# First block marked from the ranks alone, weighted slots turned block by block, shift added by the first scatter

## The reference

```python
g_prob = softmax(xt @ w_rg + b_rg); g_val, g_idx = top_k(g_prob, 1)          # 1 of 4 groups
e_logits = (xt @ w_re + b_re).reshape(-1, 4, 4); e_val, e_loc = top_k(e_logits[g_idx], 2)
e_w = softmax(e_val) * g_val                                                 # two weights per token
for e in range(16):
    out += combine[:, e] * ((silu(xt @ w_gate[e]) * (xt @ w_up[e])) @ w_down[e])
```

## Time and profile before

| what | value |
|---|---|
| three runs | 1733.82, 1735.91 (median), 1738.47 us |
| profiled execution | 1732.53 us, of it the span 1730.8 us |
| busy share of the span | TensorE 91%, weight load 61%, VectorE 54%, ScalarE 30%, GpSimd 3% |
| mean granted TensorE clock | 0.964 of full speed |
| memory traffic | 547.28 MB, mean 316 GB/s |
| gate and up matmuls (line 1048) | 6016 records, 371.2 us |
| last chain by engine | TensorE 74%, SyncE's queue 15%, DMA 4%, VectorE 4% |

### The profile page before, as it was taken

How to read it: one execution, slowest core, us unless ns; L and a number is a source line. 1 busy time by engine, 2 the same in 40 slices (tenths; PEclk the granted TensorE clock), 3 DMA queues, 4 the chain that set the end, 5 groups by cost and what they waited for, 6 DMA issues and landing times.

```text
span 1730.8 us, 35353 instructions
## 1 busy us (share of the span) xinstructions
PE 1568.8 (91%) x14820; PEld 1060.2 (61%) x14821; DVE 926.5 (54%) x1444; ACT 522.8 (30%) x602; POOL 48.4 (3%) x36
## 2 busy tenths in 40 slices
PE   8999999997999999966699999999989999986664
PEld 8999899885444444322299999998744444432221
DVE  7658655646555555431477476466475554552234
ACT  4552543423121212110264543533232112111011
POOL 0004000000000000000000040000000000000000
PEclk9999999999999999988899999999999999998887
DMA  9553455588999999999975544555999999999996
GB/s 305 202 179 126 160 167 189 195 337 351 420 422 422 418 419 400 424 421 422 410 235 180 162 144 160 166 191 195 392 373 421 421 422 422 419 423 422 422 421 269
DMA packets 139206, 547.28 MB, mean 316 GB/s; under 512 B 23060, under 2 KB 26360, under 8 KB 88568
## 3 DMA queue, kind: packets, MB, share of 16 engines
q1 hardware_dynamic: 138740, 546.13, 80.9%
...
HBM read 544.04 MB, written 2.10 MB: 316 GB/s over the span
## 4 chain that ended last, share of the span: by engine, by line
PE 74%; SPq 15%; DMA 4%; DVE 4%; issue 2%; DVEq 1%; ACT 0%; ACTq 0%
PE ps L808 24%; PE ps L1048 14%; PE ps L965 10%; SPq L432 9%; PE ps L1066 7%; SPq L436 5%; PE ps L805 5%; PE ps L1031 4%; PE ps L1012 3%; DMA room<-in_w_down_dram 3%; PE ps L1020 1%; DVE room L1118 1%; DVE h L1118 1%; PE ps L934 1%; PE ps L884 1%
## 5 line engine op out<-in xcount | busy, mean ns | idle before, releaser
L1048 PE MATMUL ps<-room 128*32 128x256 f32 x6016 | 371.2, 404 | 96.6 <-DMA room<-in_w_up_dram 91.1
L1118 DVE TENSOR_TENSOR w_lo<-room,w_hi 128x2048 fp32r<-128x2048 f32 (+1 forms) x121 | 281.4, 2335 | 232.9 <-ACT w_hi L520 232.4
L1048 PEld LDWEIGHTS ps<-room 128*32 128x32 f32 x6016 | 201.2, 116 | 282.0 <-DMA room<-in_w_up_dram 111.6
L808 PE MATMUL ps<-hT_hi,w_hi 128*128 128x256 f32 x1152 | 330.9, 287 | 0.9 <-DVE w_lo L1118 0.7
L808 PE MATMUL ps<-hT_hi,w_lo 128*128 128x256 f32 x1152 | 327.8, 285 | 0.0
L808 PE MATMUL ps<-hT_lo,w_hi 128*128 128x256 f32 x1152 | 327.7, 284 | 0.0
L520 ACT ACTIVATE w_hi<-room 128x2048 fp32r<-128x2048 f32 x120 | 228.3, 1914 | 228.4 <-PE ps L808 102.0
L1118 DVE TENSOR_TENSOR h<-h,ps 128x512 f32<-128x512 f32 x376 | 232.9, 681 | 98.0 <-PE ps L1031 97.5
L808 PEld LDWEIGHTS ps<-hT_hi,w_hi 128*128 128x128 f32 x1152 | 223.0, 194 | 3.8 <-issue 2.4
L808 PEld LDWEIGHTS ps<-hT_hi,w_lo 128*128 128x128 f32 x1152 | 223.0, 194 | 0.7 <-issue 0.5
L808 PEld LDWEIGHTS ps<-hT_lo,w_hi 128*128 128x128 f32 x1152 | 222.9, 194 | 0.0
...
## 6 DMA issues: line engine op xcount, KB each, us to landing
room<-in_w_gate_dram SPq DMA_DIRECT2D x128, 1024.0 KB, 19.0
room<-in_w_up_dram SPq DMA_DIRECT2D x128, 1024.0 KB, 21.0
room<-in_w_down_dram SPq DMA_DIRECT2D x128, 1024.0 KB, 16.5
...
```

The lines of the kernel that those rows point to most:

```text
L808: last = eng.matmul(ps[:, b + o // 2, (o % 2) * T:(o % 2) * T + T], w_[:, o * P:o * P + P], x_[:, kk, :], start=opens and o % 2 == 0, stop ...
L1048: last = eng.matmul(ps[r0:r0 + BLK, 0, 0:2 * P], xe[:, x0:x0 + BLK], unit_gu(u)[:, :, k, c * P:c * P + P], start=(i == 0 and k == 0), stop ...
L1118: return eng.tensor_tensor(o, a, b, op)
```

## The change

- `first_hot`: right after the ranks VectorE compares the ranks within expert 0 with 0 to 31 and multiplies by the membership in expert 0. Counting, `tab_first`, sort and positions come behind it, positions and the further marks behind `take_rows`.
- The spreading of positions and weights over partitions, `rows` and `place_rows` go. For each block VectorE makes `weighed` (a one-hot of slots times weights, `weigh`), TensorE turns it with 8 matmuls (`place_block`, behind `scatter(g, 1)`), and ScalarE copies the result to `place`.
- The shift is no longer loaded to all partitions. `yraw` is cleared, four rows of it get `ln1_b`, and `place` is 1 for slot 0 of each group and 0 elsewhere, so that the scatter of block 0 adds the shift to every token.
- The gain's load moves from ahead of the units to behind the ninth. The two gain multiplications are split around `hidden(g0)`.
- `h_k` is made in two steps, the first ahead of the first half's logits; `hT_r` moves to other room for that. Two filler calls instead of nine stand behind the ranks. GpSimd's clearing of the pads waits for `tab_ready` instead of `place_last`.

```diff
 eng.wait_ge(mix_split.sem, mix_split.at(l, 4))
-for m, v in enumerate((ln1_g, ln1_b)):
-    eng.dma_start(gb[:, m, :], v[l:l + 1].to_broadcast([P, D])).then_inc(gb1_loaded.sem, 16)
 def weights(w, e):
...
     e, i = u // PER_E, u % PER_E
+    if u == SLOTS:
+        eng.wait_ge(yraw_zero.sem, yraw_zero.at(l, 1))
+        eng.dma_start(gain_1, ln1_g[l:l + 1].to_broadcast([P, D])).then_inc(gb1_loaded.sem, 16)
+        eng.dma_start(yraw[0:P:BLK, :], ln1_b[l].rearrange("(c n) -> c n", c=4)).then_inc(gb1_loaded.sem, 16)
...
     half_evac(0, b)
+by_features(0)
 logits_evac(0)
...
 logits_evac(1)
-for t in range(NT):
-    eng.activation(h_k[:, t], h[:, t, :].rearrange("a (p k) -> a k p", k=KD), ACT.Copy
-                   ).then_inc(hk_ready.sem, 1)
+by_features(1)
 eng.wait_ge(ex_in.sem, ex_in.at(l, 1))
...
 copy_of(first_gathered.sem, first_gathered.at(l, 1), xrow, 3, first_rows.sem)
-eng.wait_ge(gain_done.sem, gain_done.at(l, 1))
-eng.wait_ge(spread_done.sem, spread_done.at(l, 1))
-eng.activation(rows.rearrange("p r t -> p (r t)"), banks(4, 2), ACT.Copy).then_inc(spread_ready.sem, 1)
 eng.wait_ge(tab_first.sem, tab_first.at(l, 1))
...
     copy_of(hmT_done, g + 1, hmT, 1, hmT_ready)
+    eng.wait_ge(place_done, g + 1)
+    eng.activation(place, ps[:, 1, P:P + T], ACT.Copy).then_inc(place_ready, 1)
     copy_of(y_done, g + 1, yraw, 2, y_ready)
...
 eng.matmul(ps[:, 1, 32:48], ones[:], M[:, 2, 1, :], start=False, stop=True).then_inc(ranks_done.sem, 1)
-keep_busy(9, 7)
+keep_busy(2, 7)
 def gather(ready, count, done):
...
     if t == 0:
-        eng.wait_ge(place_ready, g + 1)
+        eng.wait_ge(place_ready, g + l + 1)
         eng.wait_ge(y_ready, g + 1)
...
                    start=True, stop=True, tile_position=(r0, 0)).then_inc(sc_done, 1)
+def place_block(g):
+    eng.wait_ge(weighed_ready, g + 1)
+    for t in range(NT):
+        for c in range(4):
+            r0 = BLK * c
+            last = eng.matmul(ps[r0:r0 + BLK, 1, P + t * P:P + t * P + P], weighed[:, t, :], ident[:],
+                              start=True, stop=True, tile_position=(0, r0))
+    last.then_inc(place_done, 1)
...
             scatter(g, 1)
+            place_block(g)
...
-for i in range(2):
-    for j, col in ((0, pos12), (1, wts)):
-        for t in range(NT):
-            last = eng.matmul(banks(4, 2)[:, (2 * j + i) * T + t * P:(2 * j + i) * T + t * P + P],
-                              col[:, i, t, :].to_broadcast([P, P]), ident[:], start=True, stop=True)
-last.then_inc(spread_done.sem, 1)
...
-eng.wait_ge(place_last.sem, place_last.at(l, 1))
+eng.wait_ge(place_ready, g0 + nb + l + 1)
 eng.wait_ge(y_ready, g0 + nb + 1)
...
             eng.wait_ge(added, (g0 + nb) * 8 + c + 13)
-        eng.matmul(ps[:, 4 - 4 * t + c, :], place_l[r0:r0 + BLK, t * P:t * P + P], yraw[r0:r0 + BLK, :],
+        eng.matmul(ps[:, 4 - 4 * t + c, :], place[r0:r0 + BLK, t * P:t * P + P], yraw[r0:r0 + BLK, :],
                    start=True, stop=True, tile_position=(r0, 0)).then_inc(sc_last.sem, 1)
...
                     ).then_inc(hr_dve.sem, 1)
+eng.wait_ge(lgp_done.sem, lgp_done.at(l, NT))
+eng.memset(yraw, 0.0).then_inc(yraw_zero.sem, 1)
 eng.wait_ge(logits_done.sem, logits_done.at(l, 1))
...
 eng.wait_ge(ranks_done.sem, ranks_done.at(l, 1))
+counts = ps[:, 1, 0:NT * 16].rearrange("p (t e) -> p t e", t=NT)
+tt(hot, iota[:].rearrange("p (o s) -> p o s", o=1).to_broadcast([P, NT, BLK]),
+   counts[:, :, 0:1].to_broadcast([P, NT, BLK]), ALU.is_equal)
+eng.drain()
+tt(hot, hot, M[:, 2, :, 0:1].to_broadcast([P, NT, BLK]), ALU.mult).then_inc(first_hot.sem, 1)
 tt(over[:], ps[:, 1, 32:48].rearrange("p (e o) -> p e o", o=1).to_broadcast([P, 16, T // BLK - 1]),
...
-tt(sorted_blocks, sorted_by, tab[:, 0:1, :].to_broadcast([P, 16, 16]), ALU.mult)
-eng.drain()
-eng.tensor_reduce(tab[:, 1, :], sorted_blocks, AX.X, ALU.add)
-eng.drain()
-eng.scalar_tensor_tensor(pos, tab[:, 1:2, :].to_broadcast([P, NT, 16]), float(BLK),
-                         ps[:, 1, 0:NT * 16].rearrange("p (t e) -> p t e", t=NT), ALU.mult, ALU.add)
-eng.tensor_copy(block_iota, iota[:])
-eng.drain()
-tt(t32[:], M[:, 0:2], pos.rearrange("p (o t) e -> p o t e", o=1).to_broadcast([P, 2, NT, 16]), ALU.mult)
-eng.drain()
-eng.tensor_reduce(pos12, t32[:], AX.X, ALU.add)
-eng.drain()
-def mark(ready):
-    tt(hot_2[:], block_iota.rearrange("p (o u s) -> p o u s", o=1, u=1).to_broadcast([P, 2, NT, BLK]),
-       pos12.to_broadcast([P, 2, NT, BLK]), ALU.is_equal)
-    eng.drain()
-    tt(hot, hot_2[:, 0], hot_2[:, 1], ALU.add).then_inc(ready, 1)
-    ts(block_iota, block_iota, float(BLK), None, ALU.add)
-    eng.drain()
-mark(first_hot.sem)
-ts(tab[:, 1, :], tab[:, 1, :], carry[:], None, ALU.add)
 eng.tensor_reduce(total[:, 0, :], tab[:, 0, :], AX.X, ALU.add)
+eng.tensor_copy(tab[:, 1, 0:1], carry[:])
+tt(tab[:, 1, 1:2], tab[:, 0, 0:1], carry[:], ALU.add)
 eng.drain()
...
                          ).then_inc(tab_first.sem, 1)
-eng.wait_ge(ex_ready.sem, ex_ready.at(l, 1))
-eng.tensor_reduce(gval, ex[:, :, 0:4], AX.X, ALU.add)
-ts(wts[:, 1], ex[:, :, 4:5], 1.0, None, ALU.add)
-eng.drain()
-eng.scalar_tensor_tensor(gval, gval, ALPHA, wts[:, 1], ALU.mult, ALU.mult)
-eng.drain()
-eng.reciprocal(wts[:, 0], gval)
-eng.drain()
-tt(wts[:, 1], wts[:, 0], ex[:, :, 4:5], ALU.mult).then_inc(wts_ready.sem, 1)
+tt(sorted_by, key.rearrange("p (o n) -> p o n", o=1).to_broadcast([P, 16, 16]),
+   key.rearrange("p (e o) -> p e o", o=1).to_broadcast([P, 16, 16]), ALU.is_gt)
+eng.drain()
+tt(sorted_blocks, sorted_by, tab[:, 0:1, :].to_broadcast([P, 16, 16]), ALU.mult)
+eng.drain()
 def take_rows(done, count):
...
     tt(x4, x4, b_, ALU.add).then_inc(xe_ready, 1)
+take_rows(first_turned.sem, first_turned.at(l, 1))
+eng.tensor_reduce(tab[:, 1, :], sorted_blocks, AX.X, ALU.add)
+eng.drain()
+eng.scalar_tensor_tensor(pos, tab[:, 1:2, :].to_broadcast([P, NT, 16]), float(BLK), counts, ALU.mult, ALU.add)
+ts(block_iota, iota[:], float(BLK), None, ALU.add)
+eng.tensor_copy(place_iota, iota[:])
+eng.drain()
+tt(t32[:], M[:, 0:2], pos.rearrange("p (o t) e -> p o t e", o=1).to_broadcast([P, 2, NT, 16]), ALU.mult)
+ts(tab[:, 1, :], tab[:, 1, :], carry[:], None, ALU.add)
+eng.drain()
+eng.tensor_reduce(pos12, t32[:], AX.X, ALU.add)
+eng.drain()
+def slots(iota_):
+    return tt(hot_2[:], iota_.rearrange("p (o u s) -> p o u s", o=1, u=1).to_broadcast([P, 2, NT, BLK]),
+              pos12.to_broadcast([P, 2, NT, BLK]), ALU.is_equal)
+def mark():
+    slots(block_iota)
+    eng.drain()
+    tt(hot, hot_2[:, 0], hot_2[:, 1], ALU.add).then_inc(hot_ready, 1)
+    ts(block_iota, block_iota, float(BLK), None, ALU.add)
+    eng.drain()
+def weigh():
+    slots(place_iota)
+    eng.drain()
+    tt(hot_2[:], hot_2[:], wts.to_broadcast([P, 2, NT, BLK]), ALU.mult)
+    ts(place_iota, place_iota, float(BLK), None, ALU.add)
+    eng.drain()
+    tt(weighed, hot_2[:, 0], hot_2[:, 1], ALU.add).then_inc(weighed_ready, 1)
+eng.wait_ge(first_gathered.sem, first_gathered.at(l, 1))
+mark()
+eng.wait_ge(ex_ready.sem, ex_ready.at(l, 1))
+eng.tensor_reduce(gval, ex[:, :, 0:4], AX.X, ALU.add)
+ts(wts[:, 1], ex[:, :, 4:5], 1.0, None, ALU.add)
+eng.drain()
+eng.scalar_tensor_tensor(gval, gval, ALPHA, wts[:, 1], ALU.mult, ALU.mult)
+eng.drain()
+eng.reciprocal(wts[:, 0], gval)
+eng.drain()
+tt(wts[:, 1], wts[:, 0], ex[:, :, 4:5], ALU.mult)
 def add_block(g, t):
...
     tt(hmid, sgate, ps[:, 0, P:2 * P], ALU.mult).then_inc(hm_ready, 1)
-def place_rows():
-    eng.scalar_tensor_tensor(place, rows[:, 0, :], slot_col, rows[:, 2, :], ALU.is_equal, ALU.mult)
-    eng.scalar_tensor_tensor(place_2, rows[:, 1, :], slot_col, rows[:, 3, :], ALU.is_equal, ALU.mult)
-    eng.drain()
-    tt(place, place, place_2, ALU.add).then_inc(place_ready, 1)
-    ts(slot_col, slot_col, float(BLK), None, ALU.add)
-take_rows(first_turned.sem, first_turned.at(l, 1))
-eng.wait_ge(first_gathered.sem, first_gathered.at(l, 1))
-mark(hot_ready)
 eng.wait_ge(gb1_loaded.sem, gb1_loaded.at(l, 32))
 eng.wait_ge(hk_ready.sem, hk_ready.at(l, NT))
-tt(h[:, 0, :], h[:, 0, :], gb[:, 0, :], ALU.mult)
-tt(h[:, 1, :], h[:, 1, :], gb[:, 0, :], ALU.mult).then_inc(gain_done.sem, 1)
-eng.tensor_copy(slot_col, slot_of[:])
+tt(h[:, 0, :], h[:, 0, :], gain_1, ALU.mult)
+ts(place, slot_of[:].to_broadcast([P, T]), 0.0, None, ALU.is_equal).then_inc(place_ready, 1)
+eng.wait_ge(tab_first.sem, tab_first.at(l, 1))
+g0, nb = expert_row(eng, 1, 0), expert_row(eng, 4, 0)
 tt(carry[:], carry[:], total[:, 0, :], ALU.add)
...
 eng.drain()
+hidden(g0)
+tt(h[:, 1, :], h[:, 1, :], gain_1, ALU.mult)
 for r0, r1 in ((0, 2), (2, 3)):
...
 tt(tabi[:, 3, FIXED:], tabf[:, 0, FIXED:], tabf[:, 1, FIXED:], ALU.add).then_inc(tab_ready.sem, 1)
-eng.wait_ge(spread_ready.sem, spread_ready.at(l, 1))
-eng.memset(place, 0.0).then_inc(place_ready, 1)
-eng.wait_ge(tab_first.sem, tab_first.at(l, 1))
-g0, nb = expert_row(eng, 1, 0), expert_row(eng, 4, 0)
-hidden(g0)
-tt(h[:, 0, :], h[:, 0, :], gb[:, 1, :], ALU.add)
```

(7 more changed lines are left out.)

48 lines of the change are left out of this document (22 added, 26 removed).

## The result

The change makes the kernel slower by 0.3%: 1743.2 us against 1736.3 us (medians of 14 runs each on one chip), ratio 1.0032, 95% interval 1.0020 to 1.0044, so +3.5 to +7.6 us with +5.6 us in the middle (the medians alone differ by 6.9 us). The forecast was 1746 us, +10.3 us: direction and range held, the size was nearly twice that of the interval's middle.

The account below looks back on a forecast made before the run. TensorE was taken to bind from the first block to the last two-block expert, transfers afterwards. Layer 0: -3.0 + 16 x 0.50 = +5.0 us; layer 1: -1.7 + 14 x 0.50 = +5.3 us; +10.3 us, 1746.2 us, range 1737 to 1754 us.

Parts of the forecast that it names:

- Start of block 0: Head of each expert stage: marks without table, sort and positions let block 0 start 3.5 us earlier in each layer.
- rival 4: Head: the first block is not earlier, as the gather waits for the second feature copy or registers; +7 us more, 1753 us; 5%.
- Block 0: First expert block: VectorE's moved work and gain wait take back 0.5 us in layer 0 and 1.8 us in layer 1.
- from the end of the row scaling ... 15.7 us: Block 0: VectorE's operations up to its first add, listed one by one, sum to 15.7 us.
- Rival 3: Block 0's gate/up runs partly at half clock after seven of nine filling calls go; 2 to 3 us more, +12 us, 1748 us; 6%.
- About 1 us of it passes VectorE's list: Block 0: of the 2 to 3 us that gate/up would lose at half clock, about 1 us outlasts VectorE's work.
- The turned slots: Each block: eight added TensorE matmuls (16 records) behind the second scatter cost 0.50 us, over 16 blocks in layer 0, 14 in layer 1.
- Nothing added there is hidden: Blocks up to the last two-block expert: TensorE works end to end, so added matmuls show in full, 0.50 us a block.
- Behind the deciding block: From block 17 (layer 0) or 15 (layer 1) only transfers count, so +5.0 and +5.3 us pass to the layer's end.
- Transfers as the limit in the blocks before (1): Expert stage: transfers bind instead of TensorE, so the earlier start and removed losses give -9.8 us, 1726 us; 7%.
- Block 0 getting short (2): VectorE reaches its first add before TensorE needs it; block 0 takes 17 us instead of 23.3 and 22.4, 1732 to 1737 us; 9%.
- Weight loads in the open (5): Turning matmuls: each of 16 weight loads stands alone at 116 ns, 1.9 us a block, +52 us, 1788 us; 3%.

Follow-up runs that it names:

- the two transposes: Changed kernel with each block's place turned by two 128 x 128 transposes instead of eight matmuls: 1743.1 us, 1.0030 to the kernel before.
- one exchanged pair of lines: Changed kernel with the second half's gain multiplication ahead of block 0's gating instead of behind it: 1737.3 us, 0.9997 to the kernel before.

## Why the forecast was right in sign and too large

**Start of block 0** (3.5 us): 3.2 and 3.4 us. The two small operations, the gather and the row scaling came as reckoned; the missing part is the registers that TensorE reads ahead of the turn, a piece of rival 4. The second feature copy ended at 407.08 us, 1.3 us ahead of the gather at 408.36 us, near the 1.5 us of the forecast. The tenth unit was issued 2.9 us behind the start and not 2 us, since gate/up was slow: 2.2 us earlier in place of 3.5.

**Block 0** (longer by 0.5 and 1.8 us; layer 0's terms give 0.4 us): 24.06 us against 23.32 and 23.18 (+0.7 to +0.9), and 23.99 against 22.38 and 23.30 (+1.6 or +0.7). The sums were near, the reason was not, so that they were near is partly luck. The step "from the end of the row scaling ... 15.7 us" took VectorE's list as the limit, with waits of 0.3 and 1.6 us for the gain; they were 0.30 and 0.96 us. What I left out is that the list stops 2.25 and 1.58 us for the gate. Rival 3 had the mechanism: gate/up at a granted clock of 0.80, 8.80 us in place of 7.11 us in both layers of the profile. I gave it 6%, and its clock came. "About 1 us of it passes VectorE's list" was right as well, 1.1 us at the second scatter; left out was the clock behind that, which makes it 2.3 us at block 1. Its total of +12 us didn't come, because the next step was wrong by more. The Trainium skill ("TensorE: Matmul & The Clock Gate", HAM oscillation) warns of what gaps between matmul groups do to the clock. The runs agree as far as they go: with waits of 0.7 to 1.2 and 1.6 us ahead of it gate/up took 8.67 to 8.80 us in 9 layer heads of 12 and 7.11 us in 3, and with fillers 7.11 us in all.

**The turned slots** (0.50 us a block): this is the term that was too large. Their price was right in kind and size, 0.46 us, and the two far bounds (nothing, and 1.9 us) were rightly given little. The Trainium skill's pair of 81 ns (same page, Back-to-back issue gap) would make them 16 x 81 ns = an estimated 1.3 us; 0.46 us is 29 ns each, so no run here shows that figure. Wrong was "Nothing added there is hidden". I had looked at one block without idle, not at the group over the whole phase, which has 2.4 us of idle for issue in 263 us. About 0.1 us of the first 16 records is hidden, of the next 16 almost nothing, of the two transposes nothing. Over 30 blocks the term was 15.0 us and is 5.1 to 5.4 + 4.4 to 5.1 = 9.5 to 10.5 us. That is 4.5 to 5.5 us, and the whole miss of 10.3 less 5.6 us (by the medians' 6.9 us the miss is 3.4 us).

**Behind the deciding block** (passes in full): block 17 to the last scatter takes 175.5 us, before 175.0 and 174.9; block 15 to it 204.8 us, before 205.3 and 205.0. Right, within 0.6 us, and so is the limit by transfers there.

**The other rivals.** Transfers as the limit in the blocks before (1) are refuted for the changed kernel by the doubled turning; they do begin to bind once block 1 starts 3 us earlier than there. In the five layers of three runs where block 1 came at 26.3 to 27.9 us, TensorE waited 1.8 to 3.3 us for weights before the deciding block; at 28.6 and 29.2 us it waited 0.2 us, and later than that not at all (with the routing unchanged). Block 0 getting short (2) needed VectorE to be ahead; the order of its list kept it from that, and one exchanged pair of lines gave it in layer 0: block 0 of 19.5 us, and a ratio of 0.9997. Weight loads in the open (5) are refuted by 0.46 us. SyncE's, GpSimd's and ScalarE's moved work cost nothing that a row shows.

**What stays open.** No version that computes the reference beats the kernel before by what the runs can tell (0.9997 to 0.9999 at best). The head's part alone with the old spreading wasn't tried, as the spreading needs the weights before block 0; nor were the gain's loads back in front. Two things aren't settled: why the idle for issue shrinks with turning matmuls in column tiles and not with two transposes, and why the clock falls in gate/up in one execution and not in the next. In layer 0 the gain is waited for 0.2 to 0.8 us in some executions and 2.0 to 2.2 us in others; no run shows what sets that.
